# The tile of norm weights takes 512 bytes a partition in place of 128

## What is computed

```python
xn = rms_norm(h, norm_mix_w)                      # nrm[:, 0, :]
hq, hf, hi, hg, fq, fk, fv, ff, ga, gb = split(xn @ w_in)
a = hgrn2_mixer(hq, hf, hi, hg, ...)              # 4 heads, chunkwise recurrence
b = fox_attention(fq, fk, fv, ff, ...)            # 8 heads, causal softmax
h = h + (sigmoid(ga) * (a @ w_a) + sigmoid(gb) * (b @ w_b)) @ w_out
x2 = rms_norm(h, norm_ffn_w)                      # nrm[:, 1, :]
# PEER: for each of 8 heads the best 16 of 128*128 experts by product keys
gates, idx = top16(x2 @ w_q, sub_keys)
h = h + sum_e gate_e * gelu(u_table[e] . x2) * v_table[e]
return rms_norm(h, norm_final_w)                  # nrm[:, 2, :]
```

## Time and profile before

| what | us |
|---|---|
| median of three runs | 1769.6 |
| lowest and highest of the three | 1761.84 and 1770.93 |
| the profiled execution | 1767.3 |
| its span, first to last instruction | 1765.4 |

### The profile page before, as it was taken

The page is one execution under the profiler, slowest core; times in us unless marked ns, Lnnn a source line. Parts: engine busy times, 40 slices in busy tenths (PEclk is TensorE's granted clock), DMA queues, the critical chain, the costliest instruction groups (busy, mean ns, idle before and its releaser), DMA issues.

```text
span 1765.4 us, 25693 instructions
## 1 busy us (share of the span) xinstructions
PE 1711.6 (97%) x9593; PEld 1601.4 (91%) x9593; DVE 1257.3 (71%) x2305; ACT 770.2 (44%) x1346; POOL 796.3 (45%) x488
## 2 busy tenths in 40 slices
PE   7899999999999999999999999998999999999996
PEld 6787877777788999999999999998999999999996
DVE  7757655753532799979899666635787878787884
ACT  4433225543321334356777677633333333333332
POOL 4535422334342778875555577783222323232310
PEclk9999999999999999999999999998999999999998
DMA  6422333265344789987877799998999999999981
GB/s 190 108 72 60 90 90 84 72 191 161 100 128 121 250 295 313 318 284 257 304 246 282 275 340 372 348 405 292 342 353 354 351 341 367 336 361 341 350 297 48
DMA packets 260995, 436.38 MB, mean 247 GB/s; under 512 B 15040, under 2 KB 184256, under 8 KB 259208
## 3 DMA queue, kind: packets, MB, share of 16 engines
q1 hardware_dynamic: 203848, 250.17, 44.0%
q0 software_dynamic: 36864, 134.23, 19.9%
q10 hardware_dynamic: 20160, 50.34, 7.6%
HBM read 373.87 MB, written 60.82 MB: 246 GB/s over the span
## 4 chain that ended last, share of the span: by engine, by line
PE 48%; issue 6%; DVE 5%; POOL 5%; DMA 3%; ACT 1%; DVEq 0%; POOLq 0%; ACTq 0%
PE bank L232 13%; PE bank L234 13%; PE bank L233 13%; PE x_rows L234 3%; PE x_rows L232 3%; PE x_rows L233 3%; POOL spl_a L227 2%; POOL rows L1193 2%; PE bank L1643 1%; DVE rows L1202 1%; DMA rows<-in_u_rows,expert 1%; DMA raw<-in_v_tab 1%; DMA raw<-in_u_t 1%; DVE hot L1428 1%; DVE lists L1456 0%
## 5 line engine op out<-in xcount | busy, mean ns | idle before, releaser
L227 POOL TENSOR_TENSOR spl_a<-raw,spl_a 128x1024 fp32r<-128x1024 f32 x171 | 414.3, 2425 | 342.1 <-ACT spl_a L223 337.8
L223 ACT ACTIVATE spl_a<-raw 128x1024 fp32r<-128x1024 f32 x296 | 313.2, 1059 | 404.8 <-PE bank L234 281.3
L232 PE MATMUL bank<-act,spl_a 128*128 128x384 f32 (+1 forms) x1216 | 428.8, 353 | 12.2 <-DVE spl_a L227 9.3
L234 PE MATMUL bank<-act,spl_a 128*128 128x384 f32 (+1 forms) x1216 | 419.0, 345 | 0.0
L233 PE MATMUL bank<-act,spl_a 128*128 128x384 f32 (+1 forms) x1216 | 418.8, 344 | 0.0
L1193 POOL DMA_INDIRECT rows<-in_v_tab,expert x128 | 145.2, 1134 | 354.4 <-DVE hot L1569 340.0
L232 PE MATMUL bank<-aws,spl_a 128*128 128x384 f32 x768 | 259.3, 338 | 6.2 <-POOL spl_a L227 6.2
L233 PE MATMUL bank<-aws,spl_a 128*128 128x384 f32 x768 | 259.0, 337 | 0.0
L234 PE MATMUL bank<-aws,spl_a 128*128 128x384 f32 x768 | 259.0, 337 | 0.0
L232 PEld LDWEIGHTS bank<-act,spl_a 128*128 128x128 f32 x1216 | 229.9, 189 | 22.7 <-DVE spl_a L227 9.3
L233 PEld LDWEIGHTS bank<-act,spl_a 128*128 128x128 f32 x1216 | 229.9, 189 | 8.5 <-issue 1.4
(11 more groups left out here) (303 smaller groups left out, 2833.0 us busy)
## 6 DMA issues: line engine op xcount, KB each, us to landing
raw<-in_u_t SPq DMA_DIRECT2D x128, 512.0 KB, 4.7
raw<-in_v_tab SPq DMA_DIRECT2D x128, 512.0 KB, 7.0
gelu_ux<-gl ACTq DMA_DIRECT2D x128, 192.0 KB, 5.1
dense_gates<-mixbuf ACTq DMA_DIRECT2D x12, 2048.0 KB, 7.5
mixbuf<-dense_gates SPq DMA_DIRECT2D x32, 768.0 KB, 9.1
mixbuf<-gelu_ux SPq DMA_DIRECT2D x32, 768.0 KB, 12.1
raw<-in_w_in SPq DMA_DIRECT2D x44, 512.0 KB, 3.8
raw<-in_w_q SPq DMA_DIRECT2D x16, 512.0 KB, 4.0
```

Source lines behind the costliest of these rows:

```text
L223: eng.activation(spl(n, 0, slice(0, W)), raw[:, s, :], ACT.Copy).then_inc(hi_done, 1)
L227: eng.tensor_tensor(spl(n, 1, slice(0, W)), raw[:, n % RAW, :], spl(n, 0, slice(0, W)).bitcast(F32), ALU.subtract).then_inc(lo_done, 1)
L232: nc.tensor.matmul(out, w_hi, x_hi, start=first, stop=False)
L234: return nc.tensor.matmul(out, w_lo, x_hi, start=False, stop=last)
```

## The change

`nrm` is allocated with 16 rows of 8 values in place of 4. The kernel uses rows 0 to 2, as before. No instruction is added, removed or moved on any engine: the five streams are row for row the same. `nrm` grows from 128 to 512 bytes a partition, so that every buffer behind it begins 384 bytes further, and what stands in front of it stays.

```diff
         cst = sb(outer, "cst", [P, 3, P])
-        nrm = sb(outer, "nrm", [P, 4, KD])
+        nrm = sb(outer, "nrm", [P, 16, KD])
         ident, ones = cst[:, 0, :], cst[:, 2, :]
```

## The result

The changed kernel takes 1757.94 us (median of 8 runs, 1756.83 to 1760.00), the kernel before 1766.01 us (8 runs, 1761.84 to 1770.93; the three shown above are among them). The ratio is 0.995, with a 95% interval from 0.9936 to 0.9964: 8.1 us less. The forecast was 4.0 us less, from 1769.6 to 1765.6, with V unchanged. What happened is rival A, V gains too, which was priced at 8.0 us less. The profiled execution took 1756.83 us.

What follows compares the result with a forecast made beforehand. PE was taken as the bound, with DMA as full in V. Terms of -4.0 us (pairs with `spl_b` or `ab_split`) and 0 for V, DMA and elements took the 1769.6 us median to 1765.6; range 1757.5 to 1777.

Steps and rivals of the forecast that it cites:

- rival A: V: 64 bytes on the other side is as good as equal, 4.0 us more gain, 1761.6 us; chance 0.20.
- What bounds the kernel: Whole kernel: PE, busy 97% of the span, so each ns between matmuls reaches the end, nearly so in the mixers.
- (1): The tile `nrm` itself: no instruction new or moved, same addresses read; cost 0.
- (5): Element operations on DVE, ACT and POOL: operands behind `nrm` move together; cost 0.
- (2): Mixers and query stage: 888 matmuls on pairs 128 bytes apart become equal, 5 ns less each; 4.0 us kept.
- the nine tenths: Mixers: share kept of the 4.4 us gain, because PE idles 13 of 312 us there; leaves 4.0 us.
- Rival C: Dear pairs: something other than their places sets them apart, so nothing moves, 1769.6 us; chance 0.14.
- (3): V: 3,072 matmuls of `aws` with `spl_a` stay 64 apart, on the other side; 0, between -4.0 and +11.4 us.
- B's end: V: upper end of the rival where the other side is as dear as 128, +11.4 us, 1777.0; chance 0.12.
- (4): DMA: packets into buffers moved off a multiple of 256 cost the same; 0, with 1 ns on short packets as bound.

Runs made afterwards that it cites:

- All but V: The changed kernel plus an unused 128-byte gap in front of `aws`, putting `aws` back to 64 past a multiple of 256; 1761.60 us, ratio 0.9968.
- V alone: The kernel before plus an unused 128-byte gap in front of `aws`, moving only `aws`, from 64 to 192 past; 1760.77 us against 1766.05.

## Why the prediction was wrong

**What bounds the kernel: right.** Each ns of distance reached the end. All but V moved the end by 4.4 us, give or take 3, where the distances alone give 4.4 to 5.3 (888 x 5 to 6 ns), and V alone by 5.3, give or take 3, where they give 4.0 (3,072 x 1.3 ns).

**(1) and (5), no cost: right as far as the traces show.** The instruction counts are the same, and PE's distances account for the 8.1 us within the scatter. The kernels with 512 and 256 bytes of `nrm` give the same time, so the tile's size plays no part.

**(2), the pairs with 512 columns: right.** The forecast was 395 to 389 or 390 ns and 4.0 us; measured were 390 and 389 ns, 5.0 us up to U on average over the traces (2.0 in the query stage, 3.0 in the mixers), and 4.4 us in the medians with this half alone. The split was misread: the prediction has 600 of the 888 products in the mixers, but 96 of the 504 of `act` with `spl_b` are output units, so it is 504 there and 384 in the query stage. By the distances of starts these are worth 2.5 and 2.1 us, and the traces show no discount for waits in the mixers: the nine tenths took 0.4 us off the sum without support from them. Rival C, nothing moves, is refuted by the same means. The rule of the Trainium skill, page "SBUF — State Buffer", section "Who interferes with whom", that PE's port for the moving operand and that for weight loads are independent and PE never waits on anyone, gives 0 for this. It does not hold as a statement on time in this kernel: the same pair takes 390 ns with equal places and 394 with a gap of 128 bytes, in the kernel where only the gap was put in.

**(3), V: the step that failed.** The term was 0, and it was -4 us: 0.1747 to 0.1733 us from start to start. That is the half of the 8.1 us that the forecast of 4.0 lacked. It rested on a row at 64 on one side and on a symmetry that no row showed ("a cost that is 0 at 0 and largest near 128 gives both sides about the same"). The map has no such shape. It repeats after 256 bytes, differs by sign (64 free and 192 dear), is not smooth (0 free, 32 dear, 64 free), and differs with the number of columns. Rows at 0, 128 and 192 could not tell the value at 64. The measured value lay on the lower bound that the prediction gave, the equal pair, so the change that rival A gave, 8.0 us, was right; A's share of 0.20 was too little and the forecast's 0.50 too much, for two values between which only an interpolation decided. The forecast's band, V within about 1.3 ns a matmul, also ended just where A lay, so the two could hardly be told apart in V's distance. What was held against A, the little room in the DMA share, was no hindrance: the share rose to 1.00 and V still gained all of it.

**A mis-sized bound in the same step.** The upper bound carried 5 ns from 512 columns over to 384. The price of 128 there is 2.6 to 2.7, or 1.3 above V before, so B's end would have been 3,072 x 1.3 = 4.0 us and not 11.4. With the dearest place, 32 or 96, 3.3 above the equal pair and 2.0 above before, it would be 6 us.

**(4), DMA: nearly right.** The price is not 0 but 1 to 2% of the queue's share and stays hidden. Comparing packets to `raw` with packets to `mixbuf` hid it, since they differ in more than the place: packets of equal size to the two kinds of place were 1 and 4 ns apart in one trace, as much as the effect or more. The 122 and 164 packets of 4,096 bytes were also an assumption, from the bytes; the earlier trace rows count 138 and 198, which would give 145 and 132 ns, so these rows couldn't settle a price of a few ns.

**The baseline.** 1769.6 was a median of three runs out of three heaps. Of eight it was 1766.0, and 1765.1 to 1770.7 in the four later series, each on a chip of its own. The forecast of 1765.6 thus was "no change" in the measure of eight runs, and rival A's 1761.6 was 3.7 us above what was measured. The change itself doesn't depend on that: 8.1 us from the eight runs, and 8.4 on the chip of the kernel with 128 bytes more.

## What to carry to other kernels

Buffer addresses are a tuning parameter of a kernel that PE bounds: put the moving operand and the weights of the longest product at the same place within 256 bytes, by padding the tiles between them. Here 128 bytes more a partition were enough, and gave 0.5%. This was measured with 128x128 weights in float32 and 384 or 512 columns; other shapes and types were not run. To find the pairs, group the matmuls by their operands and shapes and compare the means; if pairs of the same shape differ, look at the addresses of both operands. A kernel whose time moves by some tenths of a per cent after a tile was resized has perhaps only moved its buffers, so measure the same edit with a pad that keeps them in place. And a value between two measured places of such a map is not an estimate, it is unknown: write both ends.

## What was not expected of the hardware

- The distance of two matmuls depends on where their two operands lie relative to each other within 256 bytes: 173.2 to 176.5 ns with 384 columns and 227 to 234 ns with 512, with the irregular map above. Why 0 and 64 are free, and why 160 and 224 are free with 384 columns alone, no run here settles; the runs show which places, and no mechanism.
- The period is 256 bytes as far as tested: 128 and 384 bytes more are the same kernel (1757.7 and 1757.9 us), and places 128 apart, such as 64 and 192, differ.
- A DMA share of 1.00 and 351 to 355 GB/s did not hold V back: its distance goes with the difference alone, at 2,310 starts with a share of 0.99 and at 2,292 with 1.00.
- With `mixbuf`, `rows` and `gl` off a multiple of 256 the hardware queue takes 1 to 2% more of the engines for the same bytes, which stays hidden in V even at a share of 1.00.
